# Early weight splits in buffers of their own, a reworked third mixer, and square root with reciprocal for the norms

## The reference

```python
def _rms_norm(x, g):
    xf = x.astype(jnp.float32)
    y = xf * lax.rsqrt(jnp.mean(xf * xf, axis=-1, keepdims=True) + NORM_EPS)
    return (y * g).astype(x.dtype)
...
        h = h + _rms_norm(m, norm_g[layer, 1])
        f = _squared_relu_mlp(_rms_norm(h, norm_g[layer, 2]), ffn_w1[layer], ffn_w2[layer])
        h = h + _rms_norm(f, norm_g[layer, 3])
...
def forgetting_attention(qb, kb, vb, f_logit, b_forget):
...
    log_f = jax.nn.log_sigmoid(f_logit.astype(jnp.float32) + b_forget.astype(jnp.float32))
    F = jnp.cumsum(log_f, axis=1).transpose(0, 2, 1)
...
        s = jnp.einsum('bqhd,bkhd->bhqk', qi, k).astype(jnp.float32) * scale
        s = s + (Fi[..., :, None] - F[..., None, :])
        qpos = i * BLOCK + jnp.arange(BLOCK)
        s = jnp.where(kpos[None, :] <= qpos[:, None], s, -jnp.inf)
        p = jax.nn.softmax(s, axis=-1)
...
        h = rms_norm(x, norm_mix[l]) * (1.0 + sc1) + sh1
        x = x + g1 * token_mixer(h, w_in[l], b_forget[l], w_up_a[l], w_up_b[l], w_out[l])
        h = rms_norm(x, norm_ffn[l]) * (1.0 + sc2) + sh2
        x = x + g2 * swiglu(h, w_ffn_in[l], w_ffn_out[l])
    return rms_norm(x, norm_final)
```

## Time and profile before

| | |
|---|---|
| device time, median of 3 runs | 2136.08 us (2135.97 to 2136.76) |
| profiled execution: its own time | 2136.94 us |
| profiled execution: span of the profile | 2135.1 us |
| TensorE busy | 2095.5 us, 98% of the span |
| VectorE, ScalarE, GpSimd busy | 992.5, 686.1, 397.1 us |
| granted TensorE clock, mean | 0.996 |

### The profile page before, as it was taken

How to read it: one execution, slowest core, us unless ns; L and a number is a source line. 1 busy time by engine, 2 the same in 40 slices (tenths; PEclk the granted TensorE clock), 3 DMA queues, 4 the chain that set the end, 5 groups by cost and what they waited for, 6 DMA issues and landing times.

```text
span 2135.1 us, 27673 instructions
## 1 busy us (share of the span) xinstructions
PE 2095.5 (98%) x11290; PEld 1708.9 (80%) x11290; DVE 992.5 (46%) x1344; ACT 686.1 (32%) x962; POOL 397.1 (19%) x286
## 2 busy tenths in 40 slices
PE   9999999999999999999999999999999999999998
PEld 7876688888878998888888878886877788888886
DVE  5347758437254436616725333722432554332335
ACT  6356643222123323314222221524333233212211
POOL 2000017839801101001782000200000210000000
PEclk9999999999999999999999999999999999999999
DMA  6210025534522232232552232122121223322321
GB/s 220 80 60 21 21 89 159 185 117 154 182 81 89 82 107 79 80 108 80 168 187 90 97 99 99 60 89 79 44 72 45 79 79 99 108 91 87 98 99 59
DMA packets 138985, 209.46 MB, mean 98 GB/s; under 512 B 5306, under 2 KB 114040, under 8 KB 138872
## 3 DMA queue, kind: packets, MB, share of 16 engines
q1 hardware_dynamic: 129904, 180.89, 26.2%
q0 software_dynamic: 6912, 25.17, 3.6%
q10 hardware_dynamic: 2056, 1.76, 0.3%
HBM read 205.70 MB, written 2.10 MB: 97 GB/s over the span
## 4 chain that ended last, share of the span: by engine, by line
PE 91%; DVE 4%; ACT 2%; POOL 1%; issue 1%; POOLq 0%; ACTq 0%; DVEq 0%
PE ps L1918 27%; PE ps L1920 26%; PE ps L1919 26%; DVE w_lo L1281 1%; PE ps L2312 1%; PE ps L2301 1%; PE ps L2324 1%; PE ps L1973 1%; PE ps L2432 1%; PE ps L2526 1%; PE ps L2503 1%; PE ps L2504 1%; DVE h L1353 0%; POOL rstd L591 0%; PE ps L2094 0%
## 5 line engine op out<-in xcount | busy, mean ns | idle before, releaser
L1281 DVE TENSOR_TENSOR w_lo<-w_raw,w_hi 128x2048 fp32r<-128x2048 f32 x161 | 374.1, 2324 | 581.4 <-ACT w_hi L697 581.3
L1918 PE MATMUL ps<-x_hi,w_hi 128*128 128x512 f32 (+1 forms) x1408 | 547.8, 389 | 7.2 <-ACT v_ab L1166 3.9
L1920 PE MATMUL ps<-x_hi,w_lo 128*128 128x512 f32 (+1 forms) x1408 | 538.3, 382 | 0.0
L1919 PE MATMUL ps<-x_lo,w_hi 128*128 128x512 f32 (+1 forms) x1408 | 537.9, 382 | 0.0
L697 ACT ACTIVATE w_hi<-w_raw 128x2048 fp32r<-128x2048 f32 x162 | 309.7, 1912 | 524.0 <-PE ps L1920 414.4
L1918 PEld LDWEIGHTS ps<-x_hi,w_hi 128*128 128x128 f32 x1408 | 266.2, 189 | 75.1 <-issue 16.2
L1920 PEld LDWEIGHTS ps<-x_hi,w_lo 128*128 128x128 f32 x1408 | 265.2, 188 | 55.9
L1919 PEld LDWEIGHTS ps<-x_lo,w_hi 128*128 128x128 f32 x1408 | 265.5, 189 | 52.0 <-issue 0.5
L1918 PE MATMUL ps<-w_hi,h_hi 128*128 128x512 f32 x688 | 272.6, 396 | 1.3 <-DVE col_bias L1644 1.3
L1919 PE MATMUL ps<-w_lo,h_hi 128*128 128x512 f32 x688 | 272.2, 396 | 0.0
L1920 PE MATMUL ps<-w_hi,h_lo 128*128 128x512 f32 x688 | 272.1, 396 | 0.0
(11 more groups left out here) (348 smaller groups left out, 2513.7 us busy)
## 6 DMA issues: line engine op xcount, KB each, us to landing
w_raw<-in_ffn_w SPq DMA_DIRECT2D x64, 1024.0 KB, 5.4
ada_w<-in_w_ada POOLq DMA_DIRECT2D x48, 512.0 KB, 4.2
w_raw<-in_w_ffn_in SPq DMA_DIRECT2D x22, 1024.0 KB, 5.1
w_raw<-in_w_in SPq DMA_DIRECT2D x20, 1024.0 KB, 5.3
w_raw<-in_o_w_in SPq DMA_DIRECT2D x16, 1024.0 KB, 5.7
w_raw<-in_w_ffn_out SPq DMA_DIRECT2D x11, 1024.0 KB, 4.9
w_raw<-in_e_w_in SPq DMA_DIRECT2D x9, 1024.0 KB, 5.2
w_raw<-in_o_w_out SPq DMA_DIRECT2D x8, 1024.0 KB, 4.9
```

The source lines that it names most:

```text
L1281: nc.vector.tensor_tensor(w_lo[:, slot, :], w_raw[:, slot, :], w_hi[:, slot, :].bitcast(F32), ALU.subtract).then_inc(w_lo_ready, 1)
L1918: nc.tensor.matmul(dst, a_hi, b_hi, start=start, stop=False)
L1919: nc.tensor.matmul(dst, a_hi, b_lo, start=False, stop=False)
L1920: return nc.tensor.matmul(dst, a_lo, b_hi, start=False, stop=stop_)
```

## The change

Four things are changed together.

- The first two tiles of each head are split into buffers of their own, `head_hi` and `head_lo`, which lie where data of an earlier stage is no longer needed. The split of the first no longer waits for the use of `w_hi` by older tiles, only for the start of the tail, and stands ahead of the norm's work; that of the second stands behind the first square on ScalarE and behind the second `normed` on VectorE. In the heads, `add_sum` of block 2 is moved ahead of the second `normed`, and `gained` and `joined` alternate.
- `rstds` on GpSimd goes. ScalarE takes a square root of each mean square plus EPS (`root_of`), VectorE the reciprocal (`rooted`). `root_table` makes ScalarE load the table for the square root ahead of that.
- In the third mixer ScalarE's two `take_far` come first and its `split_hi` last, VectorE's `split_lo` follows the two maxima, and TensorE waits for three parts of v in place of four. VectorE gives `s_upb` its banks ahead of its last split, once the eight products of `s_upa` are gated, and orders `mg_part` later.
- The gates of forgetting attention are split into two rows of fp32r each, `f_two` (128 partitions, of which rows 0 to 3 and 32 to 35 are not zero), and picked by `f_pick`, so that the product that adds them is one of fp32r with 128 rows in place of float32 with 4.

```diff
+        head_at = {1: (Y_ + 8, Y_ + 28, Y_ + 16, Y_ + 36), 2: (Y_, Y_ + 24, Y_ + 16, Y_ + 40),
+                   3: (Y_, Y_ + 8, Y_ + 16, E_), 4: (Y_, Y_ + 24, Y_ + 16, Y_ + 40),
+                   5: (Y_ + 8, Y_ + 28, Y_ + 16, Y_ + 36)}
...
+            def root_of(t, e, src, dst):
+                c = e % 16
+                chain.link(square_m(t, e, src, dst))
+                nc.scalar.activation(root[:, c:c + 1], ss[:, c:c + 1], ACT.Sqrt, bias=small[:, 22:23]).then_inc(squares, 1)
+
+            def root_table():
+                nc.scalar.activation(root[:, 16:17], small[:, 22:23], ACT.Sqrt)
...
+                def head_split_hi(i):
+                    act.wait_ge(w_loaded[(n + i) % 2], loaded(n + i))
+                    nc.scalar.activation(head_hi[p, i][:, :], w_raw[:, (n + i) % 2, :], ACT.Copy).then_inc(w_hi_ready, 1)
+
+                act.wait_ge(mm_done, st.done + st.count - 2)
+                if p == 5:
+                    act.wait_ge(mg_ready, DK)
+                head_split_hi(0)
+                root_table()
                 sum_square(0)
+                head_split_hi(1)
                 sum_square(1)
                 h_square(0)
                 h_square(1)
-                split_hi(n, n % 2, loaded(n), st.done + st.count + 1)
-                if not partial:
-                    sum_square(2)
+                sum_square(2)
                 turned_hi(p, 0)
-                if partial:
-                    sum_square(2)
                 sum_square(3)
-                split_hi(n + 1, (n + 1) % 2, loaded(n + 1), st.done + st.count + 3)
                 h_square(2)
                 h_square(3)
                 turned_hi(p, 1)
...
-            n = S["s_small"].first + 1
-            split_hi(n, n % 2, loaded(n), S["s_va"].done + 6)
             take_far(2)
-            exp_scores(0)
             take_far(3)
+            exp_scores(0)
             act.wait_ge(far_turned, 4)
             exp_scores(1)
+            n = S["s_small"].first + 1
+            split_hi(n, n % 2, loaded(n), S["s_va"].done + 6)
...
+            def rooted(e):
+                c = e % 16
+                dve.wait_ge(squares, e + 1)
+                chain.link(nc.vector.reciprocal(rstd[:, c:c + 1], root[:, c:c + 1]))
...
                 normed(0, e + 2)
+                if partial:
+                    add_sum(pass_no, 2)
                 normed(1, e + 3)
-                split_counted(n)
+                head_split_lo(p, 1)
                 turned_lo(p, 0)
-                for t in (2, 3):
-                    if partial:
-                        add_sum(pass_no, t)
+                if partial:
+                    add_sum(pass_no, 3)
                 for t in (2, 3):
                     gained(t)
-                for t in (2, 3):
                     joined(t)
                 normed(2, e + 6)
                 normed(3, e + 7)
-                split_counted(n + 1)
                 turned_lo(p, 1)
...
+                nc.vector.tensor_tensor(f_pick[:, :], ident[:, 0:4], ident[:, 32:36], ALU.add)
+                chain.link(nc.vector.tensor_scalar(f_two[:, :], causal_row[:, :], 0.0, None, ALU.mult))
+                chain.link(nc.vector.tensor_copy(f_two[0:4, :], fa))
+                nc.vector.tensor_tensor(f_two[32:36, :], fa, f_two[0:4, :].bitcast(F32), ALU.subtract).then_inc(f_made, 1)
...
             take_up(N_S + 2)
-            split_filled(N_S + 2)
+            dve.wait_ge(upa_gated, DK)
             dve.wait_ge(bank_free, 4 + S["s_upa"].unit)
             dve.sem_inc(bank_free, DK)
+            split_filled(N_S + 2)
...
-                if f >= 2:
+                if f in (2, 3):
                     mg_part(f - 2)
-            mg_part(DK - 2)
-            mg_part(DK - 1)
+            for f in range(2, DK):
+                mg_part(f)
...
-                    nc.tensor.matmul(ps[:, s, 0:n], ident[0:4, hd:hd + 1].broadcast_to([4, P]), f_row[0:4, 0:n],
+                    nc.tensor.matmul(ps[:, s, 0:n], f_pick[:, hd:hd + 1].broadcast_to([P, P]), f_two[:, 0:n],
                                      start=False, stop=True).then_inc(a_scored, 1)
...
-            pe.wait_ge(far_ready, 4)
+            pe.wait_ge(far_ready, 3)
             for j, k in filler.during(0):
                 fill(j, k)
+            pe.wait_ge(far_ready, 4)
```

More of the change, by code:

```diff
@@ L151, in program @@
         rstd = sb("rstd", [P, 16])
+        root = sb("root", [P, 17])
         neg_half = sb("neg_half", [P, 1])
@@ L251, in program @@
         causal_row = place("causal_row", [P, SEQ], W_)
+        f_two = place("f_two", [P, SEQ], W_ + 2, F32R)
         s_prob = place("s_prob", [P, 2, SEQ], E_)
@@ L262, in program @@
         bad = place("bad", [P, 3, 256], Y_ + 55)
+        head_at = {1: (Y_ + 8, Y_ + 28, Y_ + 16, Y_ + 36), 2: (Y_, Y_ + 24, Y_ + 16, Y_ + 40),
+                   3: (Y_, Y_ + 8, Y_ + 16, E_), 4: (Y_, Y_ + 24, Y_ + 16, Y_ + 40),
+                   5: (Y_ + 8, Y_ + 28, Y_ + 16, Y_ + 36)}
+        head_hi, head_lo = [{(p, i): place(f"head_{kind}{p}{i}", [P, TILE], at[2 * i + (kind == "lo")], F32R)
+                             for p, at in head_at.items() for i in range(2)} for kind in ("hi", "lo")]
         ps = ctx.enter_context(nc.psum_tensor("ps", [P, 8, 512], F32))
@@ L578, in _ @@
                                                base=0, pattern=[[-1, P]], channel_multiplier=1))
+            nc.gpsimd.memset(small[:, 22:23], EPS)
             nc.gpsimd.memset(ones[:, :], 1.0).then_inc(consts_made, 1)
[L581 to L592, removed]
             for t in range(NT):
@@ L774, in sum_square @@
                         act.wait_ge(m_added, m_adds[pass_no] + t + 1)
-                        square_m(t, e + 2 * (t // 2) + t, m[:, t, :], bank_pair(t)).then_inc(squares, 1)
+                        root_of(t, e + 2 * (t // 2) + t, m[:, t, :], bank_pair(t))
                     else:
                         act.wait_ge(mm_done, sum_done(pass_no, t))
-                        square_m(t, e + 2 * (t // 2) + t, bank_pair(t), m[:, t, :]).then_inc(squares, 1)
+                        root_of(t, e + 2 * (t // 2) + t, bank_pair(t), m[:, t, :])
                 def h_square(t):
                     act.wait_ge(h_ready, h_before + t + 1)
-                    square_m(t, e + (2 * (t // 2) + 2 if partial is not None else 0) + t, h[:, t, :], m[:, t, :]).then_inc(squares, 1)
+                    root_of(t, e + (2 * (t // 2) + 2 if partial is not None else 0) + t, h[:, t, :], m[:, t, :])
+                def head_split_hi(i):
[6 more added lines that the diff above has]
+                root_table()
                 sum_square(0)
+                head_split_hi(1)
                 sum_square(1)
@@ L1327, in turned_lo, with head_split_lo @@
                     o.then_inc(x_ready, 1)
+            def head_split_lo(p, i):
+                n = S[HEADS[p]].first + i
+                dve.wait_ge(w_hi_ready, n + 1)
+                nc.vector.tensor_tensor(head_lo[p, i][:, :], w_raw[:, n % 2, :], head_hi[p, i][:, :].bitcast(F32),
+                                        ALU.subtract).then_inc(w_lo_ready, 1)
             def split_counted(n):
```

47 lines of the change are left out of this document (23 added, 24 removed).

## The result

The changed kernel takes 2077.61 us in the median of 4 runs (2076.55 to 2082.44), the kernel before 2136.42 beside it (2135.97 to 2136.98). The ratio is 0.9719, with a 95% interval of 0.9705 to 0.9733.

The account below looks back on a forecast made before the run. TensorE, busy 98% of the span, was taken as the bound. Gains of 9.1 + 5.4 + 1.5 + 7.3 + 0.4 = 23.7 us gave 2113.2 against the profiled execution, 2112.4 against the median (predicted); range 2107 to 2120.

Parts of the forecast that it names:

- the five places: Where gains were forecast: forgetting gates 9.1 us, third mixer's start 5.4, `s_upb` 1.5, heads 7.3, last norm 0.4.
- Gates: Forgetting attention, L2504: sixteen float32 gate products go from 11.7 to 2.6 us as fp32r; gain 9.1, bounds 8.7 to 9.4.
- L2504's successor near 2.6 us on the chain: Sign expected in the profile after: the new fp32r gate products take about 2.6 us on the chain, where they took 11.7.
- Third mixer and `s_upb`: TensorE's wait for the last v copy goes, gain 5.4 us; the wait ahead of `s_upb` shrinks, gain 1.5.
- The term for the clock: Third mixer's first filler: without the standstill its 24 products run at full clock, 5.5 us instead of 7.2, gaining 1.7.
- Heads and norms: Heads gain 2.7 us in head 2, 2.5 in 4, 1.5 in 5, 0.3 each in 1 and 3; last norm 0.4.
- The last norm: At the kernel's last norm, root and reciprocal replace an addition and GpSimd's power: gain 0.4 us.
- rival 1: Forgetting units don't follow, or the 128-row product is as slow as float32: gain 2 to 4 us, 2118; chance 8%.
- rival 2: The heads give nothing, the splits' gain being lost to the earlier addition and delayed squares: 2120 us; chance 6%.
- rival 3: Five new ScalarE table loads of 1.28 us fall between total and square: 6.4 us more, 2119; chance 4%.
- rival 4: Slower: in the heads, ScalarE's second split waits for the next tile's load and holds the other engines: 2140 us; chance 2%.
- rival 5: All of TensorE's waits go, in the heads and at `s_upb`: 2108 us; chance 8%.

Follow-up runs that it names:

- experiment 1: Kernel before plus two unused tensors that put `f_row` and the arena 128 bytes higher, weights unmoved: 2106.08 us, ratio 0.9838.
- experiment 2: Changed kernel with all its instructions, but `root` and `f_pick` housed so that `f_row` and the arena keep their old place: 2112.26 us, ratio 0.9865.
- experiment 5: Kernel before with `att_stat` declared ahead of `w_raw`, so weights and small tensors lie 128 bytes higher and the arena stays: 2106.75 us, ratio 0.9844.
- experiment 6: Kernel before with an unused tensor of 128 bytes ahead of `w_raw`, so weights and arena all move together: 2139.8 us, ratio 0.9994.
- experiment 10: Changed kernel with `w_raw` 128 bytes higher, off the common place, and `w_hi`, `w_lo` and the arena all 256 bytes higher: 2077.71 us, ratio 0.9702.
- experiment 3: Kernel before with an unused tensor of 256 bytes ahead of `f_row`, so `f_row` and the arena lie 256 bytes higher: 2140.7 us, ratio 0.9997.
- experiment 11: Kernel before with only the sixteen forgetting-attention gate products changed to `f_pick` and `f_two`, other tensors at old places: 2131.19 us, ratio 0.9954.
- experiment 14: Kernel before with the changed norms, the heads' early splits and the order around them, tensors at old places: 2129.49 us, ratio 0.9946.
- experiment 12: Kernel before with only the norms' roots moved to ScalarE's square root and VectorE's reciprocal, tensors at old places: 2138.12 us, ratio 0.9985.

## Why the prediction was wrong

**The step that failed** is the frame of the sum, not a term in it. "Against its time that is 2113.2" takes every one of TensorE's products outside the five places as unchanged, at the 0.23 us of the earlier trace rows. The prediction even named "products that take longer than they need" as a third source of time, and then looked for them in L2504 alone. The change declares `root = sb(...)` and `f_pick = sb(...)`, lines that the excerpt of the diff does not show, and they were read as names; what they do to the place of all that is declared behind them was not asked. Experiments 1, 2, 5, 6 and 10 show the cause: it is the place alone, 34.7 us without the change, 34.6 with it. What it put at nothing was 59 - 24 = 35 us. The trace of before does not show which places are fast, but a hint was there: at the 1.2 GHz level it has these products 0.43 us apart (1469.77 and 1470.20 us), half of which would be 0.21 at the full clock, an estimate from these two starts, and they came 0.23 apart.

**The planned parts** were right in mechanism and, by the traces, nearly in size. Against the kernel before beside it, experiment 2 gave 28.9 us (25.7 to 32.1), where the sum had 23.7. But the kernel before took 4 us more there. Between the two profiled executions, at mean granted clocks of 0.996 and 0.997, the spans differ by 2135.1 - 2111.7 = 23.4 us. That experiment 2's 2112.26 us is the predicted 2112.4 is luck in part, for the same reason. Experiment 3's trace shows how such a difference comes about without any gain or loss of the schedule: same instructions as before, mean clock 0.994, span 2138.4. Below, "by place" is what TensorE gains across one place, its instructions matched one by one between the trace of before and that of the experiment; together these are 25.0 us.
- Gates: 9.1 forecast, 9.8 (6.6 to 13.1) measured, 8.8 by place. "L2504's successor near 2.6 us on the chain" was too low all the same. On experiment 11's chain from 1560 to 1662 us its line (now L2510) has 5.4%, 5.5 us:

```profile
by line: PE ps L1924 22.7%; PE ps L1926 22.2%; PE ps L1925 22.1%; PE ps L2509 11.5%; PE ps L2547 5.6%; PE ps L2532 5.4%; PE ps L2510 5.4%; PE ps L2553 1.5%; PE ps L2558 1.4%; PE ps L2566 1.2%; PE ps L2514 0.6%; PE ps L2518 0.6%
```

  From the product's start to the next instruction's, the sixteen took 11.7 us before and take 4.0, not 2.6, a gain of 7.7. The other 1.1 came one step later: the instruction behind them needs 2.3 us to its successor's start in place of 3.4. One unit of 384 columns, before and in experiment 11 (the old product counts as two; 0.84 us becomes 0.28, then 0.33 becomes 0.24):

```profile
1602.21 0.91 PE L2504 MATMUL ps<-f_row,ident 4*128 4x384 f32 x2
1603.05 0.50 PE L1918 MATMUL ps<-x_hi,w_hi 128*128 128x512 f32 x1
1603.38 0.39 PE L1919 MATMUL ps<-x_lo,w_hi 128*128 128x512 f32 x1
```

```profile
1601.49 0.44 PE L2510 MATMUL ps<-f_two,f_pick 128*128 128x384 f32 x1
1601.77 0.40 PE L1924 MATMUL ps<-x_hi,w_hi 128*128 128x512 f32 x1
1602.01 0.39 PE L1925 MATMUL ps<-x_lo,w_hi 128*128 128x512 f32 x1
```

- Third mixer and `s_upb`: 6.9 forecast, 8.6 (5.4 to 11.6) measured, 5.3 + 1.4 by place. There was no half-rate clock and no gap ahead of the filler, and the second filler did not wait for VectorE's split. The term for the clock, 1.7, was 1.4 (7.0 - 5.6). It can come back a little later: experiment 2's trace has 3.4 us at a granted clock of 0.50 from 1471.9 us, behind a wait of 1.0 us for `s_prob_t`.
- Heads and norms: 7.7 forecast, 11.6 (7.9 to 15.2) measured, 9.5 by place: 0.3, 3.2, 0.3, 3.5 and 1.8 in heads 1 to 5, 0.4 in the last norm. From first total to last part, head 2 went from 703.92 - 671.57 = 32.35 us to 29.07: 3.3, forecast 2.7. In head 4 it went from 1368.64 less the first total's start, which before was this,

```profile
1333.85 1.22 DVE L1383 TENSOR_TENSOR m<-m,ps 128x1024 f32<-128x1024 f32 x1 [4.17 <-PE ps L1920]
```

  34.79 us, to 31.28: 3.5, forecast 2.5, with the 1 to 2 us wait on the normalised block that was forecast (1.44). In head 5 the last part follows its transposes after 0.84 us where it took 2.20; that is 1.4, where the forecast's 1.5 counted 1.1 for it and 0.5 for an earlier start. So heads 2, 4 and 5 gave 1.8 us more than I had worked out. The clock's return in head 4, which the prediction had in its bounds, comes in some executions only: none in the changed kernel's trace, 3.4 us at 0.51 from 1339.9 us in that of experiment 10.
- The last norm, from the square's start to the last multiplication's, took 2130.80 - 2128.67 = 2.13 us and takes 1.71, 0.4 less, as forecast. After:

```profile
2068.77 1.16 ACT m L720 x2
2069.95 0.30 ACT root L725
...
2070.48 1.28 DVE m L1933
```

**The rivals.** 1 and 2 are out by experiments 11 and 14. Of 3, the Trainium skill's page "ScalarE: Activation LUTs" (Table sets: the hidden batching unit) warned; the five extra loads, 1283 ns each in the trace, cost nothing that can be seen, since experiment 12, which has them all, is faster than before. 4 did not happen: TensorE's waits name no load. Nor did 5: 5.5 us of waits on the normalised block are left. None of the five had a mechanism outside the edited places, and that is the gap in the list.

## What to carry to other kernels

A declaration is an edit: when a change adds or resizes a tensor, list which others move, and compare one row of an untouched product by form (mean ns, same count) ahead of any explanation by waits. Before tuning waits of a few microseconds in a kernel that streams thousands of fp32r products of 512 columns, read the addresses of the stationary and of the moving operands in the built program, and try a gap that makes them equal modulo 256: it costs one run. With 256 columns another distance was best here. Time an A-B comparison of schedules with every tensor at the same place modulo 256, or the place will be booked to the schedule.

## What the runs showed of the chip

- Products of fp32r with 512 columns start 227.0 ns apart in the mean where both operands lie at the same address modulo 256, and 233.3, 231.6 and 232.7 where they are 32, 64 and 128 bytes off; other distances were not run. It is so where all other engines stand still, too. For 256 columns the order is another: 119.9 ns at 0 bytes, 119.0 at 32, 118.8 at 128, and 115.9 at 64.
- The Trainium skill's page "TensorE: Matmul & The Clock Gate" (Back-to-back issue gap) has 216 ns as the gap of one product of 512 columns by itself at the full clock, worked out from the columns. It has 131 ns for a stream of weight loads and such products, and names no type beside it. Neither is met by the fp32r products here: the trace comes to 227 at best. The Trainium skill's page "SBUF — State Buffer" (Operand start alignment) asks that an operand start at a multiple of its element's size, which every place tried here does. It speaks of what is allowed and not of speed; one such place against another is 1.6% of the kernel (34.7 us of 2140).
- Open: why the distance counts at all, which two reads of TensorE meet if that is the reason, and why a product in step pays beside one out of step only where w streams. A tile in its own place for the 256-column heads, 64 bytes off x, was not timed.
